# The first stages of a two-block transformer kernel: x read in turned form, another order of transfers, query pieces in free banks

## The reference

```
h  = x
hn = rmsnorm(h, norm_mix[0])              # x * rsqrt(mean(x^2) + eps) * gain
q, k, v = split(hn @ attn_w_qkv)          # 1024 -> 3 * 1024, 16 heads of 64
s  = q @ k.T / 8 + rel_bias[head, distance]   # masked by chunks of 64 tokens
h  = h + softmax(s) @ v @ attn_w_o
h  = h + relu(rmsnorm(h) @ w1)^2 @ w2
...                                       # five more stages of the same kind
```

## Time and profile before

| | |
|---|---|
| median of 3 runs | 1002.58 us |
| profiled execution | 1003.32 us |
| its span in the trace | 1001.5 us |
| outside the span | 1.82 us |
| PE busy | 994.0 us, 99% |
| DVE busy | 683.1 us, 68% |
| ACT busy | 555.9 us, 56% |
| POOL busy | 34.5 us, 3% |

### The profile page before, as it was taken

One profiled execution on the slowest core, in us unless ns is written; L12 is line 12 of the kernel. 1 busy time (PEld: TensorE's weight loads), 2 busy tenths in 40 slices (PEclk: granted clock), 3 DMA queues, 4 the chain that ended last, 5 costly groups with the idle time before them and its releaser, 6 DMA issues.

```text
span 1001.5 us, 14148 instructions
## 1 busy us (share of the span) xinstructions
PE 994.0 (99%) x5620; PEld 859.1 (86%) x5620; DVE 683.1 (68%) x925; ACT 555.9 (56%) x804; POOL 34.5 (3%) x37
## 2 busy tenths in 40 slices
PE   9999999999999999999999999999999999999997
PEld 7988788888889988888888888888888788888886
DVE  5777676665667897756666767665668867666564
ACT  6678654444446866444444655545467655545453
POOL 1000010000002300000000100000010010000000
PEclk9999999999999999999999999999999999999999
DMA  9943375565563545655665565765625455765621
GB/s 335 311 158 127 127 262 190 192 212 184 170 207 107 191 154 202 232 190 168 205 209 174 169 215 192 223 202 185 202 86 147 130 197 169 240 210 168 210 85 43
DMA packets 124559, 184.80 MB, mean 185 GB/s; under 512 B 3162, under 2 KB 103182, under 8 KB 124366
## 3 DMA queue, kind: packets, MB, share of 16 engines
q1 hardware_dynamic: 122304, 176.70, 53.5%
q0 software_dynamic: 1728, 6.60, 1.8%
q10 hardware_dynamic: 462, 0.60, 0.2%
HBM read 182.81 MB, written 1.07 MB: 184 GB/s over the span
## 4 chain that ended last, share of the span: by engine, by line
PE 97%; DVE 2%; ACT 0%; issue 0%; POOL 0%; DVEq 0%; POOLq 0%
PE bank L1560 37%; PE bank L1506 28%; PE bank L1513 14%; PE bank L1495 4%; PE bank L1497 3%; PE bank L1498 3%; PE bank L1586 1%; PE bank L1735 1%; PE bank L1681 1%; PE bank L1711 1%; PE bank L1695 1%; DVE w_lo L829 1%; DVE work L1006 0%; PE bank L1880 0%; PE bank L1881 0%; PE bank L1882 0%
## 5 line engine op out<-in xcount | busy, mean ns | idle before, releaser
L829 DVE TENSOR_TENSOR w_lo<-raw,w_hi 128x2048 fp32r<-128x2048 f32 x164 | 374.0, 2289 | 129.4 <-ACT w_hi L426 128.4
L426 ACT ACTIVATE w_hi<-raw 128x2048 fp32r<-128x2048 f32 x164 | 311.6, 1908 | 33.9 <-PE bank L1560 31.0
L1506 PE MATMUL bank<-xT,w_hi 128*128 128x512 f32 x1216 | 294.0, 390 | 0.0
L1506 PEld LDWEIGHTS bank<-xT,w_hi 128*128 128x128 f32 x1216 | 224.6, 188 | 43.8
L1513 PEld LDWEIGHTS bank<-xT,w_lo 128*128 128x128 f32 x1216 | 159.8, 191 | 8.4
L1513 PE MATMUL bank<-xT,w_lo 128*128 128x256 f32 x1216 | 162.3, 282 | 0.0
L1560 PE MATMUL bank<-w_hi,z_hi 128*128 128x512 f32 x472 | 153.2, 393 | 0.2
L1560 PE MATMUL bank<-w_lo,z_hi 128*128 128x512 f32 x472 | 152.0, 390 | 0.0
L1560 PE MATMUL bank<-w_hi,z_lo 128*128 128x512 f32 x472 | 151.7, 390 | 0.0
L470 ACT ACTIVATE work<-bank 128x256 f32<-128x256 f32 x152 | 49.8, 379 | 170.6 <-PE bank L1513 170.6
L1560 PEld LDWEIGHTS bank<-w_hi,z_lo 128*128 128x128 f32 x472 | 88.6, 188 | 18.9
(11 more groups left out here) (213 smaller groups left out, 770.9 us busy)
## 6 DMA issues: line engine op xcount, KB each, us to landing
raw<-in_w SPq DMA_DIRECT2D x64, 1024.0 KB, 5.3
raw<-in_f_gate SPq DMA_DIRECT2D x22, 1024.0 KB, 5.3
raw<-in_f_up SPq DMA_DIRECT2D x22, 1024.0 KB, 6.0
raw<-in_f_down SPq DMA_DIRECT2D x22, 1024.0 KB, 4.9
raw<-in_w_in SPq DMA_DIRECT2D x11, 1024.0 KB, 5.6
raw<-in_w_qkv SPq DMA_DIRECT2D x9, 1024.0 KB, 9.0
raw<-in_w_o SPq DMA_DIRECT2D x4, 1024.0 KB, 4.9
raw<-in_rec_w_o SPq DMA_DIRECT2D x4, 1024.0 KB, 5.0
```

The lines of the kernel that those rows point to most:

```text
L426: e.activation(*by_channel(n, w_hi[n % RING], raw[n % RAW]), ACT.Copy).then_inc(hi_done, 1)
L829: e.tensor_tensor(low_, here, high, ALU.subtract).then_inc(lo_done, 1)
L1506: e.matmul(bank[i], whi[:, k, b * P:(b + 1) * P], xT[:, k, :, :].rearrange("p b s -> p (b s)"), start=(k == 0), stop=False, skip_group_che ...
```

## The change

It touches the first 45 us. What it does:

- x comes a second way: `x_turned`, turned by the host, with `norm_mix[0]`'s gain in its first 8 columns, in 4 parts (block 0 with the gain; block 1; blocks 2 and 3; blocks 4 to 7) into the place that `kT` takes later. The 2 + 16 transposes on PE at the start go. DVE makes `xT_hi` of blocks 0 and 1, ACT of 2 to 7.
- The vectors come ready as `cols`, in a transfer that ACT issues after its work on piece 0.
- Piece 0 comes in 4 quarters; piece 3 by halves too. SP's order is: x part 0, quarters 0, 1, x part 1, quarters 2, 3, x part 2, piece 1's halves, x part 3, pieces 2 and 3 by halves, 4, 5, then x by tokens into `h` (1 MB), the first half of the bias (1 MB), 6, 7, 8, the second half of the bias, 9 and on.
- The bias table is lengthened by the host; DRAM scratch, its write and two copies go. POOL masks each half (`bias_done` 1 and 2).
- ACT's list from piece 4: an exponential, `hi(4)`, `hi(5)`, the four squares, four evictions, `hi(6)` ... DVE's: `lo(4)`, `small_steps`, `lo(5)`, `variance`, `diags`, `spread`, `lo(6)` ...
- Query pieces m = 0, 1, 2 go to banks 4, 5, 6 and wait for no eviction; m = 3 waits for all four. `spread(L0)` stands half way in piece m = 1. The first `apply_normed` waits for `qk_leave(2)`.
- 34 warming matmuls in place of 32.

```
 sync:
+    e.dma_start(x_home[:, here], A["x_turned"][:, here]).then_inc(x_in[i], 16)
...
             else:
                 e.dma_start(dst, src).then_inc(landed[n % RAW], 16)
+                if n == N_QK + 1:
+                    e.dma_start(h, A["x"].rearrange("(t p) c -> p t c", p=P)).then_inc(h_in, 16)
+                    bias_part(0)
+                elif n == N_QK + 4:
+                    bias_part(1)
 scalar:
-        e.wait_ge(cols_done, 1)
-        hi_half(0)
-        hi_half(1)
-        x_hi(L0, 1)
-        hi_part(0, 1)
+        hi_quarter_of(0)
+        hi_quarter_of(1)
+        hi_quarter_of(2)
+        hi_quarter_of(3)
+        e.dma_start(cols, A["cols"]).then_inc(in_cols, 16)
         x_hi(L0, 2)
         x_hi(L0, 3)
         for kk in range(2):
             hi_part(1, kk)
         for k in range(4, KB):
             x_hi(L0, k)
-        for kk in range(2):
-            hi_part(2, kk)
-        hi(3)
+        for n in (2, 3):
+            for kk in range(2):
+                hi_part(n, kk)
+        e.wait_ge(sp_step, 2)
+        e.activation(sp[2], sp[1], ACT.Exp).then_inc(sp_exp, 1)
+        hi(4)
+        hi(5)
         for half in range(2):
             for t in range(T):
                 square(L0, half, t)
-        e.wait_ge(sp_step, 2)
-        e.activation(sp[2], sp[1], ACT.Exp).then_inc(sp_exp, 1)
-        hi(4)
         for t in range(T):
             e.wait_ge(v_closed, t + 1)
             e.wait_ge(rstd_done, SPREAD[L0])
...
-        hi(5)
         hi(6)
 vector:
+        x_hi_first(0)
         x_lo(L0, 0)
-        lo_half(0)
-        lo_half(1)
+        lo_quarter_of(0)
+        x_hi_first(1)
         x_lo(L0, 1)
-        lo_part(0, 1)
+        lo_quarter_of(1)
+        lo_quarter_of(2)
+        lo_quarter_of(3)
...
-        variance(L0)
-        diags(L0)
+        e.wait_ge(in_cols, 16)
         sp0().then_inc(sp_step, 1)
         e.wait_ge(sp_step, 1)
         e.tensor_tensor(sp[1], a_, sp[0], ALU.min).then_inc(sp_step, 1)
         lo(4)
         small_steps()
         lo(5)
+        variance(L0)
+        diags(L0)
         spread(L0)
         lo(6)
         e.wait_ge(rms_done, SPREAD[L0])
 tensor:
-            n, dst = N_QK + m, bank[1 + m % 3]
-            e.wait_ge(v_done, [2, 3, 4][min(m, 2)])
-            if m >= 3:
+            n, dst = N_QK + m, qk_bank(m)      # bank[4 + m] if m < 3 else bank[1 + m % 3]
+            if m == 3:
+                e.wait_ge(v_done, 4)
+            elif m >= 6:
                 e.wait_ge(qk_left, m - 2)
...
         qk_piece(0)
-        qk_piece(1)
+        e.wait_ge(consts, 4)
+        qk_piece(1, (lambda: spread(L0), nothing))
         qk_piece(2, (lambda: scores(a1, 0), nothing))
```

More of the change, by code:

```diff
@@ L37 @@
 LOOK = RING - 1
-HALVED = 3
-WARM = 32
+HALVED = 4
+WARM = 34
 HALF = D // 2
@@ L383, in x_part, with bias_part @@
         def x_part(i):
-            here = slice([0, 2 * P, HALF][i], [2 * P, HALF, D][i])
-            e.dma_start(h[:, :, here], A["x"].rearrange("(t p) c -> p t c", p=P)[:, :, here]).then_inc(x_in[i], 16)
+            here = slice(X_ENDS[i], X_ENDS[i + 1])
+            e.dma_start(x_home[:, here], A["x_turned"][:, here]).then_inc(x_in[i], 16)
+        def bias_part(i):
+            heads = slice(i * N_HEADS // 2, (i + 1) * N_HEADS // 2)
+            rows = bass.AP(tensor=A["er"].tensor, offset=A["er"].offset + heads.start * ER,
+                           ap=[[1, P], [ER, N_HEADS // 2], [1, S]])
+            e.dma_start(bias[:, heads, :], rows).then_inc(in_bias[i], 16)
         x_part(0)
@@ L400, in sync @@
             if n == 0:
[L401 to L404, removed]
+                for i in range(4):
+                    here = slice(i % 2 * HALF, (i % 2 + 1) * HALF)
+                    e.dma_start(dst[:, i // 2, here], src[:, i // 2, here]).then_inc(
+                        landed_quarter[i] if i < 3 else landed[0], 16)
+                    if i == 1:
+                        x_part(1)
+                x_part(2)
             elif n < HALVED:
@@ L431, in hi_part, with hi_quarter_of @@
             e.activation(w_hi[n][:, here], raw[n][:, here], ACT.Copy).then_inc(hi_done if kk else hi_first, 1)
[L433 removed]
+        def hi_quarter_of(half):
             here = slice(half * HALF, (half + 1) * HALF)
[L435 to L436 removed]
+            e.wait_ge(landed_quarter[half] if half < 3 else landed[0], 16)
+            e.activation(w_hi[0][:, here], raw[0][:, here], ACT.Copy).then_inc(hi_quarter if half < 3 else hi_done, 1)
         def x_hi(j, k):
[L439 to L440 removed]
+            if j:
+                e.wait_ge(turned, KB * (j - 1) + k + 1)
+            else:
+                e.wait_ge(x_in[2 if k < 4 else 3], 16)
+            e.activation(xT_hi[:, k, :], turn_banks[j][k % 4][:, 0:S] if j else x_raw[:, k, :], ACT.Copy,
                          scale=gains[j][:, k:k + 1]).then_inc(xhi_done, 1)
@@ L446, in square @@
             else:
-                for part in ((2,) if half else (0, 1)):
-                    e.wait_ge(x_in[part], 16)
+                e.wait_ge(h_in, 16)
             i = 2 * half + t
@@ L1115, in vector @@
             x_lo(L0, k)
[L1116 to L1121, removed]
-        variance(L0)
-        diags(L0)
+        for n in (2, 3):
+            for kk in range(2):
+                lo_part(n, kk)
+        e.wait_ge(in_cols, 16)
         sp0().then_inc(sp_step, 1)
@@ L1433, in gpsimd @@
         e.memset(minus_half, -0.5).then_inc(consts, 1)
[L1434 to L1437, removed]
         e.wait_ge(consts, 5)
         rstds(L0)
[L1440 to L1444, removed]
+        for i in range(2):
+            e.wait_ge(in_bias[i], 16)
+            e.memset(bias[0:CHUNK, i * N_HEADS // 2:(i + 1) * N_HEADS // 2, 0:CHUNK], NEG).then_inc(bias_done, 1)
         e.wait_ge(var_done, M0 + 1)
@@ L1719, in tensor @@
             e.matmul(bank[3][:, 0:P], zeros, zeros, start=True, stop=True)
[L1720 to L1723, removed]
-            e.transpose(bank[0][:, g * P:g * P + rows], vec_rows[0:rows, g, :], ident[0:rows, 0:rows]).then_inc(
-                vec_turned, 1)
-        for k in range(2):
-            turn(L0, k)
         def v_products(n, kk, halves, x_low, w_low, first):
```

124 lines of the change are left out of this document (63 added, 61 removed).

## The result

The changed kernel took **1005.13 us** (median of 21 runs, 1003.96 to 1006.05), the kernel before 1002.98 us beside it (21 runs, 1002.47 to 1004.06): ratio **1.0019 [1.0013, 1.0026]**. That is 2.7 us over the forecast of 1002.4 and outside its range of 999.6 to 1004.5; against the kernel before beside it the change made the kernel 2.15 us slower, where 0.2 us faster was forecast. The profiled execution of after took 1004.02 us, of which 1002.2 are its span.

A forecast was written before the change was run, and what follows sets the result against it. PE was taken as the bound from 11 us on (97% of the chain). A start 3.8 us earlier, less 3.55 of waits for ACT's and DVE's lists, left 0.2 us gained: 1002.4 us, range 999.6 to 1004.5.

The forecast's parts named there:

- The signs of being wrong: Up to 54 us: scores starting before 44, ACT waiting for DMA at hi(6) or hi(9), or PE still waiting after 54.
- The start: PE's first product at 5.1 us, v ending at 27.6 (26.9 to 28.2) against 31.40: 3.8 us earlier.
- rival 4: The start doesn't come earlier: quarter 0 at 4.7, v at 28.5; ACT's list hides it, still 1002.4; 3%.
- The other list: Three-engine chain from piece 4's landing: lo(6) starts at 38.2 instead of 37.1, qk_leave(1) at 43.2.
- the term for piece 4's landing: Start of the chain to lo(6): piece 4 lands at 21.3 us, bounds 20.2 and 22.5.
- These are ready 2.05 after `qk_leave(1)` starts: Before PE's scores: they are ready at 45.25 us, where PE wants them at 43.3.
- What PE sees: PE waits 0.85 at m = 2, 1.9 at the scores, 0.8 at the second turning: 3.55 of the 3.8 given back.
- rival 1: No give-back: PE keeps the 3.8 us of the earlier start, 998.8 us; 8%.
- The step from profile to median: Whole kernel: profiled execution forecast at 1003.1 us, less the 0.74 it lay above the median before, gives 1002.4.
- h, the bias, piece 9: SP's queue: h about 27, first bias half about 30, both covered; piece 9 about 45, may land up to 46.3.
- rival 2: Bias halves in SP's queue delay piece 9, to 51 if each takes twice 2.97: 1007 us; 9%.
- Rival 3: Each transfer costs the queue its own time, delaying piece 4: 1004.4 us at a third of the price, 1008 at all; 3%.

The follow-up runs named there:

- e2_h_first: Changed kernel with x by tokens (h, 1 MB) sent ahead of piece 4 instead of behind piece 5; 1007.07 us, ratio 1.0043.
- e3_reorder: Changed kernel with small_steps moved to the first feed-forward, lo(6) ahead of spread, second bias half sent behind piece 9; 1001.28 us, ratio 0.9983.
- again: The changed kernel run once more, nothing altered; 1004.98 us, ratio 1.0020.
- e10: Changed kernel with only the second half of the bias sent behind piece 9 instead of ahead of it; 1004.73 us, ratio 1.0018.
- f2: Changed kernel with 11 small matmuls on zeros ahead of piece 1, in PE's early 1.3 us wait; 1004.46 us, ratio 1.0019.
- e1_swap: Changed kernel with small_steps moved behind variance and diags in DVE's list; 1003.81 us, ratio 1.0008.
- e6_aligned: Changed kernel with the 8 gain columns of x_turned padded to 64; 1004.19 us, ratio 1.0015.
- f1_fill_scores: Changed kernel with 20 small matmuls on zeros in PE's waits, 4 before m = 2 and 16 before the scores; 1004.00 us, ratio 1.0009.

## Why the prediction was wrong

The mechanism (an earlier start, given back by the lists of DVE and ACT) was right, two of its terms were too small, one cost was missing, and the largest error was the last step, from the profiled execution to the median. The miss of 2.7 us splits so: the profiled execution took 1004.02 where 1003.1 was forecast (0.9), and the median, taken as 0.74 below it, was 1.11 above it (1.8). The signs of being wrong that the prediction listed did not give it away: the scores started at 46.22, ACT waited for no transfer at `hi(6)` or `hi(9)`, and PE's last wait ended at 54.16, with the turning itself.

**The start.** First product at 4.86, forecast 5.1: right. End of v 28.56, forecast 27.6: the waits inside were 1.3 at piece 1 instead of 0.7 at quarter 1 and its low part. For the end of v this was rival 4's case (28.5), though quarter 0 came in time, and as that said, the lists hide it: e2_h_first and e3_reorder move the turning by 3.0 one way and 2.5 the other without an edit to PE's start.

**The other list: the term for piece 4's landing.** Every duration in it held: small steps 4.9, `lo(5)` 2.2, `variance` to diagonals 1.27 (34.39 - 33.12), `lo(6)` to `qk_leave(1)` 5.01. Its origin did not: piece 4 landed at 21.84, and `hi(4)` behind it started between 21.58 and 23.25 in the other profiles of kernels with this order up to piece 4 and no padding, where 21.3 was taken. I reckoned "the same 5 MB" minus 90 KB at the old rate; between 4.5 and 8.5 us, now full of small transfers, DMA moved only 237 GB/s for 331. That is +0.5, inside the bounds that the text gave, but the value sat at the favourable end of what was measured. Why the rate dips is open; padding may be a part of it and didn't settle it.

**"These are ready 2.05 after `qk_leave(1)` starts".** They were ready 2.45 after (45.74 + 0.42 - 43.71): +0.4, so the turning came 10.45 behind it instead of 10.05. It was taken over from the earlier trace rows as if it were fixed, and why it changed isn't shown. 0.5 and 0.4 are the 0.9.

**What PE sees.** Waits of 0.85, 1.9 and 0.8 were forecast; 0.5, 2.0 and 0.7 came. So the give-back, the core of the forecast, is shown, and rival 1 is excluded; e3_reorder shows what keeping the gain needs: not shorter operations, as the rival said, but another order.

**The missing cost: what a 2 us wait does to PE's clock.** The text priced PE's waits at their length. In two of the eight profiles that keep the 2.0 us wait the granted clock stands at half for about 3.4 us, at once when PE starts again in one and 2 us later in the other. The turning then comes 32.8 behind `hi(4)` (54.10 - 21.34; 54.43 - 21.68) instead of 32.3: 0.45 us, after PE's later wait has swallowed part. That the wait lowers the clock is shown by the counts above, 33 of 76 runs against 0 of 132. What it costs the median is not. In after, **again**, e10 and f2 the runs below 0.998 have medians 0.8 to 1.0 above the others, in e1_swap 0.3, and the two of e6_aligned lie under the rest. With the 20 fillers the kernel lies 1.0 above before instead of 2.1, but only 0.5 under f2_fill_early of its own batch; 16 fillers gave e1_swap its clock back and no time; and the intervals of the ratios of f1_fill_scores and after overlap. So it is somewhere between nothing and 1.2 us. The Trainium skill (TensorE: Matmul & The Clock Gate, "Part 1: The HAM clock gate") says that the gate passes half of the pulses when PE has lately been idle and all when it has been busy; these rows agree on the two levels, 0.50 and 1.00, and show that the same wait leaves the clock at 1.00 in six other profiles.

**The step from profile to median: the largest error.** Subtracting 0.74 because before's profiled execution lay that far above its median was no more than a guess of one draw. It failed on both sides. The median of three runs of before was itself 0.40 low: 21 runs give 1002.98, and the profiled execution lies 0.34 above that. And after's profiled execution, one at full clock, was the third fastest of its 21. Of the 1.11 from there to the median, the 7 runs of low clock make 0.4 (without them the median is 1004.7), and a typical landing of piece 4 some 0.1 to 0.3 (median 21.96 and mean 22.1 over the ten profiles with this order and no padding, for 21.84). The rest, about half, stays open.

**h, the bias, piece 9.** `hi(6)` and `hi(9)` (45.67) didn't wait for DMA: rival 2 is out. Rival 3, each transfer costing the queue its own time, is out at the prices that it named: with three more transfers ahead of it piece 4 landed 0.3 us later than before (21.84 for 21.5) and 0.5 later than forecast, where a third of the price made 2 us and all of it 6. A small price, up to 0.2 us each, isn't excluded, since the early rate fell and its cause is open.

## What to carry to other kernels

When a change frees the engine that bounds, write down the lists of the others from their first outside event, here the landing of one transfer, and bound that landing by measured scatter; everything behind it moves one for one. Work with a late due time (24 small steps, a copy that only a later operation wants) should be moved off that list before the start is made faster: the same change was 0.19% slower without that and, with the small steps, `spread` and one `lo` placed later, 0.23% faster. A wait of 2 us on TensorE can cost more than its length (0.45 us more in two profiles); price it with the clock at half behind it. And don't take the distance of one profiled execution from the median of three runs as a constant: it was 0.74, 0.34 with 21 runs, and -1.11 for the changed kernel.

## What the runs showed of the hardware

- After 2.0 us without a matmul PE ran at a granted clock of 0.50 for about 3.4 us in two profiles (from 45.7 us on, at once, in e6_aligned; from 48.0, with 2 us of work at full clock ahead of it, in e10_bias_only) and at 1.00 in six others of the same wait. With the wait halved by fillers, or gone, no run has a mean clock below 0.998 (132 runs; 33 of 76 with the wait). The waits of up to 1.6 us during v showed no such fall in any of the fourteen profiles, and filling one changed neither clocks nor time measurably (f2_fill_early).
- The landing of one and the same transfer differed by up to 1.7 us between executions (`hi(4)` from 21.58 to 23.25). In the kernels whose DVE list is that of after, the turning followed it (32.3 us behind `hi(4)` in six of eight profiles, 32.8 in the two with the clock at half).
- One wait of DVE for ACT took 1.00 us in eight kernels and 0.58 to 0.59 in four with the same operations around it; its cause was not found.
